# Interleaving 96-place and 64-place expert groups in a mixture-of-experts layer

## The reference, cut to what matters

```python
h2 = rmsnorm(x, g_ffn)                      # 512 x 1024
idx, wts = route(h2, w_router, router_bias) # 8 of 64 experts for each token
x = x + routed_experts(h2, idx, wts, w_exp_gate, w_exp_up, w_exp_down) \
      + swiglu(h2, w_sh_gate, w_sh_up, w_sh_down)
...
def swiglu(x, wg, wu, wd):
    return (jax.nn.silu(x @ wg) * (x @ wu)) @ wd
```

## Time and profile before

| | |
|---|---|
| time, median of 3 runs | 1059.02 us (1058.03, 1059.02, 1060.67) |
| span of the profiled execution | 1058.3 us |
| the profiled execution's own time | not listed apart; 0.7 us more than its span brings it to the median of the runs |
| first to last step of the experts | 396.1 to 961.2 us of the span |
| TensorE busy | 963.5 us, 91% |
| bytes moved | 292.87 MB |
| mean granted TensorE clock | 0.971 |

### The profile page before, as it was taken

How to read it: one execution, slowest core, us unless ns; L and a number is a source line. 1 busy time by engine, 2 the same in 40 slices (tenths; PEclk the granted TensorE clock), 3 DMA queues, 4 the chain that set the end, 5 groups by cost and what they waited for, 6 DMA issues and landing times.

```text
span 1058.3 us, 15067 instructions
## 1 busy us (share of the span) xinstructions
PE 963.5 (91%) x6147; PEld 433.8 (41%) x6147; DVE 288.1 (27%) x652; ACT 161.2 (15%) x293; POOL 168.7 (16%) x320
## 2 busy tenths in 40 slices
PE   5999999999999899999999999999988887882598
PEld 4554554444444343343333333333323222330487
DVE  3322641002212562344322111111101010110982
ACT  2002230150000101111111111211111111210111
POOL 3235000000001011222222222222221212101100
PEclk9999999999999899999999999999989998996699
DMA  9351211121231818999999999999999999988931
GB/s 334 126 159 42 78 40 53 68 79 40 87 143 36 361 53 325 379 401 407 416 408 413 417 408 405 397 406 373 421 422 421 420 422 421 417 368 306 402 157 40
DMA packets 70692, 292.87 MB, mean 277 GB/s; under 512 B 8204, under 2 KB 30240, under 8 KB 43616
## 3 DMA queue, kind: packets, MB, share of 16 engines
q1 hardware_dynamic: 57872, 255.96, 61.1%
q0 software_dynamic: 12176, 33.86, 8.3%
q10 hardware_dynamic: 576, 2.10, 0.5%
HBM read 275.63 MB, written 25.69 MB: 285 GB/s over the span
## 4 chain that ended last, share of the span: by engine, by line
PE 72%; DMA 22%; DVE 3%; SPq 1%; issue 1%; ACT 1%; POOL 0%; POOLq 0%; DVEq 0%
PE ps L1705 21%; DMA ring<-in_w_exp_up 19%; PE ps L1433 11%; PE ps L1733 8%; PE ps L1813 5%; PE ps L1535 5%; PE ps L1417 3%; PE ps L1377 3%; PE ps L1520 3%; PE ps L1518 3%; PE ps L1354 3%; DMA ring<-accumulator 2%; PE ps L1581 2%; PE ps L1383 1%; PE ps L1566 1%
## 5 line engine op out<-in xcount | busy, mean ns | idle before, releaser
L1705 PE MATMUL ps<-ring,gates 128*32 128x512 f32 x2624 | 298.5, 608 | 34.0 <-DMA ring<-in_w_exp_up 32.5
L1705 PEld LDWEIGHTS ps<-ring,gates 128*32 128x32 f32 x2624 | 91.4, 112 | 235.1 <-issue 233.3
L1733 PE MATMUL ps<-ring,poolbuf 128*32 128x512 f32 x1312 | 149.3, 595 | 1.7 <-ACT actT L768 0.9
L1204 DVE COPY poolbuf<-ps 128x256 f32<-128x256 f32 x41 | 17.4, 425 | 412.8 <-PE ps L1716 412.8
L1433 PE MATMUL ps<-actT,ring 128*128 128x512 f32 x256 | 112.3, 595 | 0.0
L597 POOL TENSOR_TENSOR tickets<-cst 128x1 f32<-128x1 f32 x79 | 14.9, 189 | 393.6 <-ACT actT L768 387.9
L1733 PEld LDWEIGHTS ps<-ring,poolbuf 128*32 128x32 f32 x1312 | 38.8, 109 | 88.7 <-issue 87.4
L1433 PEld LDWEIGHTS ps<-actT,ring 128*128 128x128 f32 x256 | 47.9, 190 | 59.6 <-issue 59.5
L768 ACT ACTIVATE actT<-ps,qT 128x1024 f32<-128x1024 f32 x41 | 45.7, 1114 | 149.2 <-PE ps L1733 149.2
L1354 PE MATMUL ps<-cst,rows 128*128 128x128 f32 x392 | 53.1, 281 | 13.0 <-DMA cst<-in_constants 10.2
L558 POOL TENSOR_SCALAR st<-st 128x1 f32<-128x1 f32 (+2 forms) x17 | 7.4, 434 | 337.2 <-ACT rows L730 241.9
(11 more groups left out here) (226 smaller groups left out, 849.4 us busy)
## 6 DMA issues: line engine op xcount, KB each, us to landing
ring<-in_w_exp_gate SPq DMA_DIRECT2D x64, 1024.0 KB
ring<-in_w_exp_up SPq DMA_DIRECT2D x64, 1024.0 KB, 18.6
ring<-in_w_exp_down SPq DMA_DIRECT2D x64, 1024.0 KB, 14.7
ring<-accumulator SPq DMA_DIRECT2D x16, 1024.0 KB, 11.9
ring<-in_w_gate SPq DMA_DIRECT2D x8, 1024.0 KB, 13.1
ring<-in_w_in SPq DMA_DIRECT2D x5, 1024.0 KB
ring<-in_w_out SPq DMA_DIRECT2D x4, 1024.0 KB
ring<-in_w_ple_gate SPq DMA_DIRECT2D x4, 1024.0 KB
```

The costliest lines, as they stand in the source:

```text
L1705: last = mm(bank(2 + k)[part, :], hgT[k][:, q, part], pair_view(EXPERT_SLOT[js[c]])[:, q], start=(q == 0), stop=(q == KD - 1))
L1733: last = mm(bank(6 + half)[part, :], eactT[r % 2][:, q, part], w[:, q, half * 512:(half + 1) * 512], start=(q == 0), stop=(q == 1))
```

## The change

The same 9 big and 7 small groups are worked on in another order: B S B S B S B S B S B S B B B S (groups 0 to 15). `IS_BIG` holds it, `cap_of`, `STEP_OF` and the load order read it. A group keeps its experts: the big ones come in the order of falling counts as before, and so do the small ones. `first_sorted(g)` gives the rank of the first expert of group g; it is written into 64 new columns of the constant table (`C_SORTED`), and `perm` compares with them in place of 0 to 63. The table loses the 128 columns of ones, which a memset makes on the chip. `JOB_AT` and the number of steps stay.

```diff
-STEP_OF = [(g, s) for g in range(NGROUP) for s in range(GROUP * (CAP if g < BIG_GROUPS else CAP2) // P)]
+IS_BIG = [g % 2 == 0 or g == NGROUP - 3 for g in range(NGROUP)]
+STEP_OF = [(g, s) for g in range(NGROUP) for s in range(GROUP * (CAP if IS_BIG[g] else CAP2) // P)]
...
 def cap_of(g):
-    return CAP if g < BIG_GROUPS else CAP2
+    return CAP if IS_BIG[g] else CAP2
+
+def first_sorted(g):
+    alike = sum(1 for q in range(g) if IS_BIG[q] == IS_BIG[g])
+    return GROUP * (alike if IS_BIG[g] else BIG_GROUPS + alike)
...
-    c[:, C_ONE:C_ONE + P] = 1
...
+    for g in range(NGROUP):
+        c[:, C_SORTED + g * GROUP:C_SORTED + (g + 1) * GROUP] = first_sorted(g) + np.arange(GROUP)
...
                 if e:
                     in_used(step)
                     load_in(pos, e[0])
-                    if g - 1 >= BIG_GROUPS:
+                    if not IS_BIG[g - 1]:
                         load_in(pos + 1, e[1])
                 if late:
                     down_used(step - 1)
                     load_down(pos - 2, late[0])
                     load_down(pos - 1, late[1])
-                if e and g - 1 < BIG_GROUPS:
+                if e and IS_BIG[g - 1]:
                     in_used(step + 1)
...
-            nc.vector.tensor_copy(oneT[:, :], cst[:, C_ONE:C_ONE + P])
+            nc.vector.memset(oneT[:, :], 1.0)
...
-            nc.vector.tensor_scalar(perm, cst[0:NE, C_IOTA:C_IOTA + NE], pos_col, None, ALU.is_equal
+            nc.vector.tensor_scalar(perm, cst[0:NE, C_SORTED:C_SORTED + NE], pos_col, None, ALU.is_equal
...
-                own = cst[:, C_PAIR:C_PAIR + 6] if g < BIG_GROUPS else cst[:, C_PAIR2:C_PAIR2 + 4]
+                own = cst[:, C_PAIR:C_PAIR + 6] if IS_BIG[g] else cst[:, C_PAIR2:C_PAIR2 + 4]
```

More of the change, by code:

```diff
@@ L57 @@
 JOB_AT = 24
-C_ID, C_SLT, C_ONE = 0, P, 2 * P
-C_IOTA = 3 * P
+C_ID, C_SLT = 0, P
+C_IOTA = 2 * P
 C_IOTA8 = C_IOTA + CAP
@@ L70 @@
 C_IC = C_PAIR2 + 4
-C_ALL = C_IC + NG * PAD
+C_SORTED = C_IC + NG * PAD
+C_ALL = C_SORTED + NE
 def cap_of(g):
-    return CAP if g < BIG_GROUPS else CAP2
+    return CAP if IS_BIG[g] else CAP2
+def first_sorted(g):
+    alike = sum(1 for q in range(g) if IS_BIG[q] == IS_BIG[g])
+    return GROUP * (alike if IS_BIG[g] else BIG_GROUPS + alike)
 def steps_of(g):
@@ L111, in constant_table @@
     c[0:NE, C_KEYP] = key
-    for g, at in ((0, C_PAIR), (BIG_GROUPS, C_PAIR2)):
+    for g, at in ((IS_BIG.index(True), C_PAIR), (IS_BIG.index(False), C_PAIR2)):
         for step in range(steps_of(g)):
```

## The result

The changed kernel is slower. Its median is 1069.88 us (5 runs), that of the kernel before 1060.67 us in the same session; the ratio is 1.0084, 95% interval 1.0061 to 1.0107. In a later session, beside the last experiments, it was 1072.54 us against 1059.65, a ratio of 1.0122 (1.0104 to 1.0141). So the cost is 9 to 13 us. Forecast were 1061.6 us and a range up to 1067.5: a cost of 2.6 us. The sign of the sum was right, its size too small by a factor of three to five, and the time lies above the range.

A forecast was written before the change was run, and what follows sets the result against it. DMA and TensorE bound the expert stage in turn; the tail eats the 11.4 us win, leaving step 40 at 942.6. Adding 0.8 + 2 + 0.5 - 0.1 gives 945.8, span 1061.0, forecast 1061.6 us, range 1056 to 1067.5.

The forecast's parts named there:

- The tail: Steps 30 to 40, big groups carrying jobs: bound by TensorE at 13.47 us a step, 134.7 us, eating the whole win.
- The win: Expert stage up to step 30: alternating groups keep the DMA queue deeper, at 421 GB/s; 11.4 us to win.
- the 12.1 us of lack: From 430.2 to 770.8 us the kernel before moves 406 GB/s, not 421; the time so lost is 12.1 us.
- 0.7 + 0.8 + 2: Lack kept before step 30: 0.7 us before the orders differ, 0.8 us shallow queue until about step 8, 2 us dips.
- the dips: Queue runs low before a big group's last release: 0.4 us for each of five big groups, 2 us in all.
- rival 3: Shallow queues: dips of 1.1 us each, 5.5 us, and group 12 delayed by 2.8 us; 1067.7 us, chance 0.25.
- a wait that isn't there now: Big group behind a small one: first down product waits for its matrix, hidden up to step 30; 0.5 us allowed.
- The count at step 30: Step 30 starts once 18 more loads and 1.6 MB of rows, 20.5 MB or 48.6 us, have moved: at 807.9.
- The clock: TensorE's waits move ahead, partly slowing the next input product; 1.7 us per wait over 2 us, hidden by the DMA.
- Rival 4: Cold clock: three waits a pair slow input products to 8.77 us; 3.3 us more ahead of step 30, 1065 us, chance 0.07.
- Rival 2: Real gain: last load's landing, not TensorE, sets the end; step 40 at 931.7, 1047.6 us, chance 0.05; weaker form near 1055, 0.05.

The follow-up runs named there:

- e8: Changed kernel with only an eighth of the rows gathered (14.7 MB less for the DMA, leaves out work): 1046.94 us, ratio 0.9872.
- e2: Changed kernel with the sixteen jobs at steps 16 to 31 in place of 24 to 39: 1061.90 us, ratio 1.0011.
- e4: Kernel before (old order) with the sixteen jobs at steps 16 to 31: 1071.23 us, ratio 1.0104.
- e13: Changed kernel with the order six big, seven small, three big groups, so no turns: 1080.51 us, ratio 1.0174.
- e3: Changed kernel, but behind a small group the next group's first two down matrices load ahead of the last input matrices: 1069.86 us, ratio 1.0080.
- e9: Changed kernel with input products of steps 3 to 29 leaving out a quarter of their sum (less TensorE work): 1069.54 us, ratio 1.0100.
- e12: Changed kernel run once more, unaltered, in a later session: 1072.54 us, ratio 1.0122.
- e5: Changed kernel with three big groups first, then small and big in turn to the end: 1060.05 us, ratio 0.9995.
- e7: Kernel before with only an eighth of the rows gathered (14.7 MB less, leaves out work): 1045.01 us, ratio 0.9859.

## Why the prediction fell short

Two steps failed: the deeper queue that was to bring the DMA to its full rate, and the count of bytes, which took an awaited load to land when all bytes ahead of it and no others had moved. Each cost some 5 us. (Of the 8.3 us between 1061.6 and 1069.88, 1.65 are the kernel before itself, whose median was 1060.67 in the same runs and not 1059.02; and 1061.0 + 0.7 is 1061.7.)

**The tail: right.** 134.7 us forecast, 134.97 measured in the changed kernel, 134.76 in e8. e2, e4 and e13 show each side of it.

**The win: the step that failed first.** "So from about step 8 on, every pair is bound by the DMA, its queue stays deeper, and the 12.1 us of lack can come back." The first half held, from step 5. The second held for 120 us (420 GB/s from 448.5 to 570) and no longer: 408 from there to step 30. By my own measure, the lack between steps 3 and 30 is 390.84 x (1 - 412/421) = 8.4 us; 0.7 + 0.8 + 2 = 3.5 us were allowed for. Mis-sized: the dips, 2 us in the sum. This is rival 3's mechanism, priced there at 5.5 us.

One such dip, around the big group 8, in TensorE's order of time and in stretches of 4 us:

```profile
698.71 5.34 PE L1742 MATMUL ps<-ring,poolbuf 128*32 128x512 f32 x32 [3.00 <-DMA ring<-in_w_exp_down]
703.83 7.08 PE L1714 MATMUL ps<-ring,gates 128*32 128x512 f32 x64
```

```profile
700.00:704.00 4.00, 4.00 (x32) 1.44 (x28) 0.00 (x0) 0.00 (x0) 0.00 (x0) 0.72 1.02 422
704.00:708.00 4.00, 4.00 (x43) 1.42 (x36) 0.00 (x0) 1.12 (x1) 1.59 (x4) 1.00 0.94 367
708.00:712.00 4.00, 4.00 (x38) 1.95 (x30) 0.62 (x2) 0.38 (x1) 1.24 (x2) 1.00 0.87 283
712.00:716.00 4.00, 3.81 (x35) 0.98 (x33) 0.73 (x2) 0.64 (x2) 0.00 (x0) 1.00 0.88 327
```

The down product waits 3.0 us for its matrix and then takes 5.34 us in place of 3.64 at the lower clock (0.72 granted); the next input product ends at 711 and only then frees the slots of experts 2 and 3. By that time the DMA has fallen to 283 GB/s. The chain of "a wait that isn't there now" was described, and judged hidden "by the DMA's backlog" up to step 30. In this group it wasn't. But e3 took the waits away and e9 gave TensorE 39 us, and neither brought the rate above 415. So late releases are shown in this dip, but by themselves they are not the whole cause of the 408; what else bears on it comes out of the next part.

**The count at step 30: the step that failed second.** 138.3 + 18.9 + 1.6 = 158.8 MB were to be moved between steps 3 and 30; the rate times the stretch gives 390.84 x 0.412 = 161.0 MB, and 160.3 to 160.8 in e3, e9 and e12. The awaited load lands when 1.5 to 2.2 MB more has moved than counted, 4 to 5 us. In e5 the same count (13 loads and 332 rows over the kernel before, 15.0 MB) is short by 1.2 MB.

The kept traces show what these bytes are. A load raises its semaphore by 16, one at a time, and the trace keeps the moment of each; I read each as the share of one of the 16 DMA engines; the trace doesn't name the engine. The load that step 30 awaits, issued at 798.11, has 15 of its 16 shares by 814.33 and the last at 819.53, 5.2 us later. By then 15, 13 and 11 shares of the three loads queued behind it have landed, 39 x 65,536 bytes = 2.6 MB, against 0.5 MB at step 3. In e12 they are 2.1 MB against 0.3, in e9 2.6 against 0.7, in e5 1.4 against 0.6; in the kernel before 0.7 against 0.8 (some of its signals are missing). The growth from step 3 to step 30 is the surplus to within 0.4 MB in each. The queue behaves as 16 queues that are unevenly far, and the prediction had put this at nothing without a reason.

The unevenness grows while the DMA has no pause. "First to last share" is the mean time over which the shares of one load land. "Without a share" is an estimate of the engine time in which no load in the queue had a share left for that engine: it counts a load from 1.6 us after its issue (the shortest time from issue to first share is 4.1 us, less eight packets of 0.31 us); with 1.0 or 2.5 us the 2.3% below becomes 1.7 or 3.6%.

| stretch | first to last share, us | last behind the 15th, us | GB/s | missing against 421 | without a share (estimate) |
|---|---|---|---|---|---|
| changed, 448.5 to 570 | 6.5 | 0.7 | 420 | 0.2% | 0.1% |
| changed, 570 to step 30 | 9.4 | 3.3 | 408 | 3.1% | 2.3% |
| e9, steps 3 to 30 | 8.5 | | 415 | 1.4% | 1.0% |
| e8, steps 3 to 30 | 7.3 | | 409 | 2.9% | 1.9% |
| e7, steps 3 to 30 | 2.1 | 0.5 | 385 | 8.6% | 7.0% |
| e13, small groups | 11.3 | 2.8 | 418 | 0.7% | 0.2% |
| changed, steps 30 to 40 | 6.6 | | 370 | 12.1% | 9.9% |

In the changed kernel the shares of a load land within 3.4 us at 430 to 450 us and within 11.3 at 570 to 590, where the first hole stands (403 GB/s from 570 to 600). In the dip above, at 710 us, the three loads in the queue have 15, 13 and 10 of their 16 shares: ten engines have nothing left, while one still holds up the oldest load. So a lead of some engines makes a late release cost more: the same queue is empty for most of them sooner. e7 has hardly any lead, and its low rate comes from the short queue alone; e13's small groups have the largest lead, but a deeper queue (6.4 loads in the mean of 570 to step 30, against 5.6 in the changed kernel), and keep 418. The estimate follows the missing rate from stretch to stretch and stays somewhat below it. But no run changed the unevenness alone, so its part in the 408 is argued and not shown by an experiment.

Together: 4.9 us of rate and 5.2 us of bytes are the 10 us by which steps 3 to 30 outlast the forecast 380.5 us. What stays open is why one share falls behind, and how the 408 divides between the lead and the late releases.

**The clock.** TensorE meets the lower clock more often, as forecast: waits of 2.84 and 3.45 us are followed by input products of 8.77 and 9.99 us, one of 2.42 us by 7.07. The Trainium skill (TensorE: Matmul & The Clock Gate, "HAM oscillation — how this bites in real kernels") says of a kernel with a wait for a transfer ahead of each piece of work that every piece starts cold. Here, of nine waits of over 2 us for an input matrix, seven are followed by a product of 8.67 to 9.99 us and two (2.35 and 2.42) by one of 7.07; and in the kernel before a wait of 3.67 us, at 927, is followed by 7.07. Its cost is hidden up to step 30 by the loads, but for what it adds to a dip.

```profile
456.16 8.77 PE L1714 MATMUL ps<-ring,gates 128*32 128x512 f32 x64 [2.84 <-DMA ring<-in_w_exp_up]
...
498.32 9.99 PE L1714 MATMUL ps<-ring,gates 128*32 128x512 f32 x64 [3.45 <-DMA ring<-in_w_exp_up]
...
601.48 7.07 PE L1714 MATMUL ps<-ring,gates 128*32 128x512 f32 x64 [2.42 <-DMA ring<-in_w_exp_up]
```

**The rivals.** Rival 3, shallow queues, came nearest with 1067.7 us: the dips are there, and deeper than its 5.5 us, but its other half, a delay of group 12, isn't: TensorE has no pause in the tail. Rival 4, the cold clock, is out: of steps 24 to 29, where it was to cost 3.3 us, only the first has a slow product (8.67 us). Rival 2, the real gain, fell with the tail; e5, which has no such tail, shows that there was next to no gain to have either. No kernel here that does the whole work beats the one before.

## What to carry to other kernels

Where a stage is bound by compute in one part and by loads in another, ask first whether the loads have idle time in the compute-bound part: here 2 to 4% of the rate was missing, and mixing the parts could return no more than that. Whatever work hides under waits (here ten of sixteen jobs) loses its cover when the order changes; look at what the last steps carry, since no later wait can hide it. A rate below that of a deep queue, not the busy share, tells that a queue runs low, and it can't be assumed to rise to the full rate because there is more to do. After a long stretch without a pause a load lands when the slowest of its 16 shares does (here up to 6 us behind the 15th), so a count of bytes gives the landing too soon, and a queue that held enough loads at first may run dry on most engines later.

## What was not expected of the hardware

The DMA share read 1.00 to 1.01 at 408 as at 420 GB/s, in stretches of over 100 us. The same 1 MiB loads moved at 420 GB/s for 120 us of turns and at 408 for the next 250. The 16 shares of one load landed within 2.1 us of each other in the mean where the DMA had pauses (e7), and within 9 to 11 us where it had none for long; the last alone was 2 to 3 us behind the 15th there, and 6 us in the load that the down product at 698.71 waits for (15 shares by 692.6, the last at 698.6). The device time of a profiled execution was 1.85 us over its span (1072.15 and 1070.3 us), where 0.7 had been taken.
